# Attention inside a decoder block: where the next head's split, the values and the first output weights stand in the order of work

## The chip, the cores and the metric

The kernel runs on one core of a Trainium2 chip, as one program. The metric is the device time of an execution in microseconds (us); lower is better. The engines are TensorE (PE, matmuls), VectorE (DVE), ScalarE (ACT), GpSimd (POOL) and SyncE (SP), which here only issues DMA transfers. They run side by side and wait for each other through semaphores.

## The reference

One decoder block over 1024 positions with 1024 features, in float32. The mixer has 16 heads of 64 features: 8 choose the 256 best keys of each query by an indexer (DSA), 8 have a forgetting bias (FoX). Cut to what matters:

```python
mod = silu(c) @ ada_w + ada_b                      # 6 vectors of 1024
sh1, sc1, g1, sh2, sc2, g2 = split(mod, 6)
h = rms_norm(x, norm_attn_g) * (1 + sc1) + sh1
q_d, k_d, v_d, iq, ik, iw, q_f, k_f, v_f, f = split(h @ w_in)
o_d = softmax(where(among_best_256, q_d @ k_d.T / 8, -inf)) @ v_d    # per head, rope on q_d, k_d
o_f = softmax(q_f @ k_f.T / 8 + cum_q - cum_k, causal) @ v_f         # per head
y = concat(rms_norm(o_d, dsa_norm_g), rms_norm(o_f, fox_norm_g)) @ w_out
x = x + g1 * y
h = rms_norm(x, norm_ffn_g) * (1 + sc2) + sh2
x = x + g2 * ((silu(h @ w_gate) * (h @ w_up)) @ w_down)
return rms_norm(x, final_norm_g)
```

## The kernel before, in words

Each engine has one program, written out by hand; its order of work is the order of the text, and the only ties between engines are semaphores. The stages are: normalisation, projection and the choice of keys (to 378 us of the span), attention (to 705 us), the output projection and second normalisation, and the feed-forward part with the last normalisation. The change lies in attention.

Attention is a loop over 128 units: 16 heads (numbered 0 to 15; the FoX heads are 0 to 7, the DSA heads 8 to 15) of 8 tiles (0 to 7) of 128 queries each. Tile t has t+1 blocks of keys, so late tiles are larger. For unit s:

- TensorE (`logits`, L1943 to L1945) makes the scores of unit s, turns the exponentials of unit s-2 (`turn`, L1926), and multiplies those of unit s-3 with the values (`values`, L1957). The scores of unit s need VectorE's pass over unit s-2.
- VectorE (`biased`, L1524) adds the bias or the choice and takes the minimum. ScalarE (`expo`, L1015) takes the exponential and copies what TensorE has turned (L1010).
- Queries and keys are split into a high and a low part, for precision. For a head hd, SyncE loads its queries and keys twice over the partitions (`load_qk`, L540, 1 MB into `Qd`, `Kd`). GpSimd's `prepare(hd)` makes two casts (L764, L765) and the low part of the keys (L767, `k_lo`). VectorE's `query_lo(hd)` (L1543, `q_lo`) makes the low part of the queries; it needs both casts, and TensorE needs both low parts for tile 0 of that head. VectorE does `query_lo(hd+1)` at tile 3 of head hd.
- GpSimd does `prepare(0)`, then three memsets (L805, of the sums `g1b`, `g2b`, `mod23`) and two copies that spread the rope angles (L807), then `prepare(hd+1)` in the loop over heads. `prepare(hd)` waits until head hd-2 has made its scores.
- The second part of the modulation vectors is summed along: in heads 4 to 11, at tiles 1, 3, 5 and 7, VectorE adds one block of `ada_w` (`modulation(n)`, L1537). SyncE loads the blocks (`load_mod`, L588, 512 KB into `adar`), two buffers, each as its buffer comes free.
- The values of four heads at a time lie in `Vn` (`load_values(g)`, L531, 1 MB): group 2 (heads 8 to 11) is loaded in SyncE's pass hd = 5, group 3 (heads 12 to 15) in the pass hd = 8, there after a wait for the product of head 7.
- Heads 4 to 6 also turn the DSA rows (`rotate`); the pass hd = 6 of SyncE stores them (L609) and waits for the store before it loads head 8's queries.
- In head 10 VectorE squares the FoX outputs (`square`, L1559), ScalarE takes the root at tile 0 of head 11 (`roots(1)`, L1020, which needs another table of the activation function than the exponential), VectorE inverts it at tile 5 of head 11 (L1591) and scales with it in head 12.
- The output weights are split by GpSimd in heads 12 to 14 (`split_out`, L729, L731). SyncE loads their blocks (L627) after the last queries.

SyncE's passes are one queue: what stands behind a wait waits too. The pass hd is:

```python
load_qk(hd + 2)
if 1 <= hd and hd + 1 < NH:
    load_cum(hd + 1)
if hd == 5:
    load_values(2)
if hd == 8:
    load_values(3)
while n_mod < min(MOD_PER_HEAD * (hd + 1 - MOD_FIRST) + 2, 4 * KT):
    load_mod(n_mod)
    n_mod += 1
```

Of the kernel before, what the change touches and what calls it, by code (L numbers as in the profile page):

```python
# [24 lines left out]
P = 128  # L25
SEQ = 1024
D = 1024
TT = SEQ // P
KT = D // P
DH = 64  # L30
NH = 8
# [157 lines left out]
def build(nc, x, c, positions, ada_w, ada_b, norm_attn_g, w_in, b_forget, dsa_norm_g, fox_norm_g,  # L189
# [14 lines left out]
    with ExitStack() as ctx:  # L204
# [274 lines left out]
        def _(sp):  # L479
# [53 lines left out]
            def load_qk(hd):  # L533
                b, first, row = hd % 2, 0 if hd < NH else 2, hd % NH * DH
                if hd >= 2:
                    sp.wait_ge(k_lo, hd - 1)
                    sp.wait_ge(q_lo, hd - 1)
                for i, dst in enumerate((Qd[b], Kd[b])):
                    for half in range(2):
                        sp.dma_start(dst[half * DH:(half + 1) * DH, :],  # L540
                                     qk_dram[first + i, row:row + DH, :]).then_inc(qk_in[b], 16)
# [56 lines left out]
            for i, dst in enumerate((g1b[0:1, :], mod23[0:1, 0, :], mod23[0:1, 1, :], g2b[0:1, :])):  # L598
                sp.dma_start(dst, ada_b[(2 + i) * D:(3 + i) * D].rearrange("(a n) -> a n", a=1)).then_inc(mod_bias_in, 16)
            n_mod = 0  # L600
            for hd in range(2 * NH - 2):
                if hd == 1:
                    sp.wait_ge(qk_pe, TT)
                    for i in range(2):
                        sp.dma_start(RX[i][:], rope_rows(i)).then_inc(rx_in, 16)
                if hd + 2 == NH:
                    sp.wait_ge(rope_d, 6)
                    for i in range(2):
                        sp.dma_start(rope_rows(i), RX[i][:]).then_inc(rope_out, 16)  # L609
                    sp.wait_ge(rope_out, ROPE_OUT)  # L610
                load_qk(hd + 2)
                if 1 <= hd and hd + 1 < NH:
                    load_cum(hd + 1)
                if hd == 5:
                    load_values(2)
                if hd == 8:
                    load_values(3)
                while n_mod < min(MOD_PER_HEAD * (hd + 1 - MOD_FIRST) + 2, 4 * KT):
                    load_mod(n_mod)
                    n_mod += 1  # L620

            for k in range(KT):
                if k >= 2:
                    sp.wait_ge(w_ready, N_PROJ + k - 1)
                else:
                    sp.wait_ge(md_done, 4 * KT - 1 + k)
                sp.dma_start(adar[:, k % 2, :], w_out[k * P:(k + 1) * P, :]).then_inc(wo_in[k % 2], 16)  # L627


            sp.wait_ge(pv_pe, UNITS)  # L630
# [74 lines left out]
        def _(pool):  # L705
# [95 lines left out]
            pool.wait_ge(cumT_ok, 2)  # L801
            prepare(0)
            pool.wait_ge(pj_pe, NC * TT)
            for dst in (g1b, g2b, mod23):
                pool.memset(dst[:], 0.0).then_inc(md_ms, 1)  # L805
            for i, angle in enumerate((cosT, sinT)):
                pool.tensor_copy(spread[i][:], angle[:].unsqueeze(2).to_broadcast([P, TT, REPS, HALF])).then_inc(spread_ok, 1)  # L807
            for hd in range(2 * NH):
                if hd + 1 < 2 * NH:
                    prepare(hd + 1)  # L810
                    if hd + 1 in ROPE_HEADS:
                        rotate(ROPE_HEADS.index(hd + 1))
                for k in range(KT):
                    if WO_HEAD[k] == hd:
                        split_out(k)
# [49 lines left out]
        def _(act):  # L865
# [157 lines left out]
            for s in range(UNITS + 2):  # L1023
                hd, t = divmod(s, TT)
                if s in ANGLE_UNITS:
                    evac_group(("C", ANGLE_UNITS.index(s)))
                if s in MOD_UNITS:
                    evac_group(("M", MOD_UNITS.index(s)))
                if s == 11 * TT:
                    roots(1)  # L1030
                if s >= 2:
                    for b in range(len(halves(P * ((s - 2) % TT + 1)))):
                        evac_group(("T", s - 2, b))
                if s < UNITS:
                    expo(s)
# [146 lines left out]
        def _(dve):  # L1182
# [383 lines left out]
            def scaled(t, kind):  # L1566

                v = O[:, t, kind * GW:(kind + 1) * GW]
                r = kind * TT + t
                dve.tensor_scalar(v, v, rstd[:, 1, r:r + 1], None, ALU.mult).then_inc(yn_ok, 1)  # L1570
# [3 lines left out]
            dve.wait_ge(pj_pe, NC * TT)  # L1574
            for s in range(UNITS):
                hd, t = divmod(s, TT)
                if t == 3 and hd + 1 < 2 * NH:
                    query_lo(hd + 1)
                biased(s)

                if t == 5 and hd >= 1:
                    normalise(hd - 1)
                if hd == 10:
                    square(t, GW, GW, (2, 1))
                if hd == 12:
                    scaled(t, 1)
                if hd == 15:
                    square(t, 0, GW - LATE, (2, 0))
                if hd == 11 and t == 5:
                    dve.wait_ge(yroot, 1)  # L1590
                    dve.reciprocal(rstd[:, 1, TT:2 * TT], stat[:, 3, TT:2 * TT]).then_inc(yrstd, 1)  # L1591
                    dve.wait_ge(yrstd, 1)
                if MOD_FIRST <= hd < MOD_HEADS and t in MOD_TILES:
                    modulation(len(MOD_TILES) * (hd - MOD_FIRST) + MOD_TILES.index(t))
                advance(CHOICE_LATE.get(s, 0))
# [521 lines left out]
```

## Time and profile before

| | |
|---|---|
| runs shown | 1511.62, 1514.23, 1506.62 us (median 1511.62) |
| profiled execution | 1509.27 us; its span 1507.6 us |
| TensorE busy | 1416.2 us, 94% of the span |
| VectorE, ScalarE, GpSimd busy | 839.3, 666.5, 709.5 us |
| mean granted clock of TensorE | 0.965 of full |
| attention stage | 378 to 705 us |

The profile is one execution, recorded by the hardware. A busy time says how long an engine had an instruction in work; what it waited for stands in the chain, in the groups of waits and in the timelines. In a timeline a row is the start, the duration, the engine, the line, the operation with its output and inputs, and in brackets how long the engine was idle before it and what ended that. Times in the text are microseconds from the start of the span.

### The profile page before, as it was taken

The page shows a single profiled execution, that of the slowest core. Times are in us where ns is not written, and L with a number is a line of the kernel's source. Part 1 is how long each engine was busy: PE and PEld are TensorE (multiplying, and loading weights), DVE is VectorE, ACT ScalarE, POOL GpSimd, SP SyncE. Part 2 cuts the span into 40 slices and gives each one's busy share as a digit, 9 for nine tenths or more (in the row PEclk, how much of TensorE's full clock was granted, in tenths as well). Part 3 has the DMA queues.
Part 4 walks back from the last instruction along what each step waited for, and adds up shares of the span by engine and source line. Part 5 has one row for each costly group of instructions (what it writes and reads, how often), then busy time and mean ns, then how long its engine had stood idle before and what let it go on. Part 6 is the DMA issues. An engine that isn't in the chain of part 4 may idle for free.

```text
span 1507.6 us, 19842 instructions
## 1 busy us (share of the span) xinstructions
PE 1416.2 (94%) x7231; PEld 1205.5 (80%) x7231; DVE 839.3 (56%) x1456; ACT 666.5 (44%) x1274; POOL 709.5 (47%) x455
## 2 busy tenths in 40 slices
PE   1899899999799999998999799999999998999998
PEld 1888678888699988987788688888888886888886
DVE  5634879996567779635455733444433343515414
ACT  4523456541466656656435443333333332423421
POOL 2331312242435322280003998888888873642640
PEclk8899999999899999898899899999999999999999
DMA  9121222241624665520411122222222226643631
GB/s 380 48 74 60 77 78 91 91 150 50 170 63 112 207 201 162 140 78 29 154 43 56 50 90 85 84 84 84 84 85 84 84 71 259 226 150 138 205 126 56
DMA packets 103915, 171.73 MB, mean 114 GB/s; under 512 B 7981, under 2 KB 58341, under 8 KB 102794
## 3 DMA queue, kind: packets, MB, share of 16 engines
q1 hardware_dynamic: 103818, 170.46, 35.2%
q8 instruction: 58, 0.95, 0.3%
q14 instruction: 39, 0.32, 0.1%
HBM read 136.81 MB, written 33.62 MB: 113 GB/s over the span
## 4 chain that ended last, share of the span: by engine, by line
PE 82%; DVE 6%; DMA 4%; issue 2%; ACT 2%; SPq 2%; POOL 1%; DVEq 0%; POOLq 0%; ACTq 0%
PE PS L1783 22%; PE PS L1784 21%; PE PS L1785 21%; PE PS L1957 7%; PE PS L1926 3%; PE PS L1944 2%; PE PS L1945 2%; DMA rawb<-in_w_down_dram 1%; PE PS L1943 1%; DMA adar<-in_ada_w_dram 1%; DVE acc L1228 1%; PE PS L1987 1%; DVE marks_c L1365 1%; DVE XLf L1672 1%; DVE LP L1524 0%
## 5 line engine op out<-in xcount | busy, mean ns | idle before, releaser
L861 POOL TENSOR_TENSOR BS<-rawb,BS 128x1024 fp32r<-128x1024 f32 x44 | 106.9, 2434 | 127.9 <-ACT BS L1144 127.9
L848 POOL TENSOR_TENSOR WS<-WSf,WS 128x512 fp32r<-128x512 f32 x110 | 162.7, 1486 | 0.7 <-ACT WS L1088 0.7
L1088 ACT CAST WS<-WSf 128x512 fp32r<-128x512 f32 x110 | 68.4, 622 | 202.0 <-POOL WSf L838 201.1
L838 POOL TENSOR_TENSOR WSf<-rawg 128x512 f32<-128x512 f32 x55 | 77.3, 1405 | 167.7 <-PE PS L1785 166.5
L1957 PE MATMUL PS<-Vn,PT 128*128 128x64 f32 x1152 | 148.6, 276 | 0.2 <-ACT PT L1010 0.2
L1957 PEld LDWEIGHTS PS<-Vn,PT 128*128 128x128 f32 x1152 | 145.1, 199 | 0.9 <-ACT PT L1010 0.3
L1783 PE MATMUL PS<-BS,AS 128*128 128x512 f32 x352 | 138.0, 392 | 6.5 <-POOL BS L861 6.2
L1783 PE MATMUL PS<-yh,WS 128*128 128x512 f32 x352 | 137.9, 392 | 2.9 <-DVE yl L1644 2.9
L1785 PE MATMUL PS<-yh,WS 128*128 128x512 f32 x352 | 137.7, 391 | 0.0
L1784 PE MATMUL PS<-BS,AS 128*128 128x512 f32 x352 | 137.5, 391 | 0.0
L1784 PE MATMUL PS<-yl,WS 128*128 128x512 f32 x352 | 137.5, 391 | 0.0
L1785 PE MATMUL PS<-BS,AS 128*128 128x512 f32 x352 | 137.4, 390 | 0.0
L1716 DVE TENSOR_TENSOR AS<-rawa,AS 128x512 fp32r<-128x512 f32 x44 | 63.5, 1445 | 127.7 <-ACT AS L1142 127.7
L1015 ACT ACTIVATE LP<-LP,nmin 128x128 f32<-128x128 f32 (+7 forms) x128 | 99.8, 780 | 55.9 <-DVE nmin L1524 53.9
L1010 ACT COPY PT<-PS 128x512 f32<-128x512 f32 (+1 forms) x192 | 85.2, 477 | 63.0 <-PE PS L1926 62.5
L1783 PE MATMUL PS<-XH,WS 128*128 128x512 f32 x264 | 104.6, 396 | 5.6 <-DVE XL L1677 5.6
L1785 PE MATMUL PS<-XH,WS 128*128 128x512 f32 x264 | 104.4, 395 | 0.0
L1784 PE MATMUL PS<-XL,WS 128*128 128x512 f32 x264 | 104.2, 395 | 0.0
L1365 DVE TENSOR_SCALAR_CACHE_REDUCE marks_c<-sel,bis 128x640 f32<-128x640 f32 (+4 forms) x134 | 102.0, 815 | 0.5
L1926 PE MATMUL PS<-ident,LP 128*128 128x128 f32 x576 | 89.2, 283 | 6.2 <-ACT PT L1010 5.2
L764 POOL CAST QT<-Qd 128x1024 fp32r<-128x1024 f32 x16 | 18.1, 1131 | 153.2 <-PE PS L1945 150.8
L949 ACT ACTIVATE PS<-sel,bis 128x896 f32<-128x896 f32 x64 | 67.6, 1056 | 48.6 <-DVE bis L1420 36.9
(306 smaller groups left out, 3516.9 us busy)
## 6 DMA issues: line engine op xcount, KB each, us to landing
rawb<-in_w_down_dram SPq DMA_DIRECT2D x44, 512.0 KB, 3.5
adar<-in_ada_w_dram SPq DMA_DIRECT2D x32, 512.0 KB, 4.4
raw<-in_w_in_dram SPq DMA_DIRECT2D x24, 512.0 KB, 3.9
rawg<-in_w_gate_dram SPq DMA_DIRECT2D x22, 512.0 KB, 4.7
rawu<-in_w_up_dram SPq DMA_DIRECT2D x22, 512.0 KB, 4.3
gu_scratch<-Cu SPq DMA_DIRECT2D x44, 256.0 KB, 2.0
rawa<-gu_scratch SPq DMA_DIRECT2D x44, 256.0 KB, 3.6
ada<-in_ada_w_dram SPq DMA_DIRECT2D x8, 1024.0 KB, 9.4
```

The source lines that it names most:

```text
L838: pool.tensor_tensor(WSf[m % N_SLOT][:], left(i, mat, a), left(i, mat, b), ALU.add if sign > 0 else ALU.subtract).then_inc(ws_sum, 1)
L848: pool.tensor_tensor(lo, WSf[m % N_SLOT][:] if b else left(i, mat, a), hi.bitcast(F32), ALU.subtract).then_inc(ws_ready, 1)
L861: pool.tensor_tensor(b[:, 1, :], rawb[m % 2][:], b[:, 0, :].bitcast(F32), ALU.subtract).then_inc(gb_lo, 1)
L1010: act.copy(PT[:, u % 2, b * BANK:b * BANK + w], src[:, 0:w]).then_inc(tp_ev, 1)
L1015: act.activation(LP[:, u % 3, 0:n], LP[:, u % 3, 0:n], ACT.Exp, bias=nmin[:, u:u + 1], scale=-1.0, accum_out=sums[:, u:u + 1]).then_inc(ex ...
L1088: act.copy(WS[m % N_SLOT][:, 0], src).then_inc(ws_hi, 1)
L1365: did(dve.tensor_scalar(marks[0][:, n_tk % 2, 0:P * (t + 1)], view(t), limit, 0.0, op, ALU.add, accum_out=col(0, t)))
L1783: pe.matmul(dst, left[0], right[0], start=first, stop=False)
L1784: pe.matmul(dst, left[0], right[1], start=False, stop=False)
L1785: return pe.matmul(dst, left[1], right[0], start=False, stop=last)
L1926: last = pe.transpose(dst[:, i * P:(i + 1) * P], src, ident[:])
L1957: last = pe.matmul(PS[:, 6 + hd % 2, t * DH:(t + 1) * DH], PT[:, u % 2, j * P:(j + 1) * P], Vn[(hd // 4) % 2][:, j, cols], start=j == 0, s ...
```

## The change

Five things are moved; no instruction is added or removed.

- GpSimd: `prepare(1)` stands ahead of the memsets and spread copies.
- VectorE: `query_lo(hd+1)` stands at tile 6 of head hd, ahead of `biased`; it was at tile 3.
- ScalarE and VectorE: `roots(1)` at tile 6 of head 11 (was tile 0), its reciprocal at tile 0 of head 12 (was tile 5 of head 11).
- SyncE: values group 2 in the pass hd = 6 (was 5), group 3 in the pass hd = 9 (was 8).
- SyncE: the first two blocks of output weights ahead of head 14's queries (were behind head 15's).

```diff
@@ SyncE
+            def load_out(k):
+                if k >= 2:
+                    sp.wait_ge(w_ready, N_PROJ + k - 1)
+                else:
+                    sp.wait_ge(md_done, 4 * KT - 1 + k)
+                sp.dma_start(adar[:, k % 2, :], w_out[k * P:(k + 1) * P, :]).then_inc(wo_in[k % 2], 16)
...
+                if hd == WO_HEAD[0]:
+                    load_out(0)
+                    load_out(1)
                 load_qk(hd + 2)
                 if 1 <= hd and hd + 1 < NH:
                     load_cum(hd + 1)
-                if hd == 5:
+                if hd == 6:
                     load_values(2)
-                if hd == 8:
+                if hd == 9:
                     load_values(3)
@@ GpSimd
             pool.wait_ge(pj_pe, NC * TT)
+            prepare(1)
             for dst in (g1b, g2b, mod23):
                 pool.memset(dst[:], 0.0).then_inc(md_ms, 1)
...
             for hd in range(2 * NH):
-                if hd + 1 < 2 * NH:
+                if 1 <= hd < 2 * NH - 1:
                     prepare(hd + 1)
@@ ScalarE
-                if s == 11 * TT:
+                if s == 11 * TT + 6:
                     roots(1)
@@ VectorE
-                if t == 3 and hd + 1 < 2 * NH:
+                if t == 6 and hd + 1 < 2 * NH:
                     query_lo(hd + 1)
                 biased(s)
...
                 if hd == 12:
+                    if t == 0:
+                        dve.wait_ge(yroot, 1)
+                        dve.reciprocal(rstd[:, 1, TT:2 * TT], stat[:, 3, TT:2 * TT]).then_inc(yrstd, 1)
+                        dve.wait_ge(yrstd, 1)
                     scaled(t, 1)
...
-                if hd == 11 and t == 5:
-                    dve.wait_ge(yroot, 1)
-                    dve.reciprocal(rstd[:, 1, TT:2 * TT], stat[:, 3, TT:2 * TT]).then_inc(yrstd, 1)
-                    dve.wait_ge(yrstd, 1)
```

How the order of instructions changes at three places. First GpSimd at the start of attention, before (the row with `qk_in1` is the first of `prepare(1)`, the row with `qk_pe` the first of `prepare(2)`):

```order
L805 MEMSET g1b 128x1024 [waits pj_pe]
L805 MEMSET g2b 128x1024
L805 MEMSET mod 128x2048
L807 COPY spread<-cosT 128x1024
L807 COPY spread<-sinT 128x1024
L764 CAST QT<-Qd 128x1024 [waits qk_in1]
L765 CAST KA<-Kd 128x1024
L767 TENSOR_TENSOR KB<-Kd,KA 128x1024 [waits qk_hi]
L764 CAST QT<-Qd 128x1024 [waits qk_pe,qk_in0]
```

and now:

```order
L770 CAST QT<-Qd 128x1024 [waits qk_in1,pj_pe]
L771 CAST KA<-Kd 128x1024
L773 TENSOR_TENSOR KB<-Kd,KA 128x1024 [waits qk_hi]
L812 MEMSET g1b 128x1024
L812 MEMSET g2b 128x1024
L812 MEMSET mod 128x2048
L814 COPY spread<-cosT 128x1024
L814 COPY spread<-sinT 128x1024
L770 CAST QT<-Qd 128x1024 [waits qk_pe,qk_in0]
```

The split of head 1 has gone ahead of five instructions. Second SyncE in the passes hd = 5 and 6, before (`Vn` is the values, `adar` the modulation blocks, `RX` the rotated rows, `bfor_in` the wait for their store):

```order
L531 DMA Vn<-v_scratch 128x8x256 [waits pv_pe]
L588 DMA adar<-in_ada_w_dram 128x1024 [waits md_done] x4
L609 DMA qk_scratch<-RX 16x8x1024 [waits rope_d]
L609 DMA qk_scratch<-RX 16x8x1024
L540 DMA Qd<-qk_scratch 64x1024 [waits q_lo,k_lo,bfor_in]
L540 DMA Qd<-qk_scratch 64x1024
L540 DMA Kd<-qk_scratch 64x1024 x2
L550 DMA CK<-cum_scratch 2x1024 [waits qk_pe]
L551 DMA CQ<-cum_scratch 2x1024
L588 DMA adar<-in_ada_w_dram 128x1024 [waits md_done] x4
```

and now:

```order
L588 DMA adar<-in_ada_w_dram 128x1024 [waits md_done] x4
L616 DMA qk_scratch<-RX 16x8x1024 [waits rope_d]
L616 DMA qk_scratch<-RX 16x8x1024
L540 DMA Qd<-qk_scratch 64x1024 [waits q_lo,k_lo,bfor_in]
L540 DMA Qd<-qk_scratch 64x1024
L540 DMA Kd<-qk_scratch 64x1024 x2
L550 DMA CK<-cum_scratch 2x1024 [waits qk_pe]
L551 DMA CQ<-cum_scratch 2x1024
L531 DMA Vn<-v_scratch 128x8x256 [waits pv_pe]
L588 DMA adar<-in_ada_w_dram 128x1024 [waits md_done] x4
```

The values have moved from ahead of pass 5's modulation blocks to between head 8's queries and pass 6's blocks. Third VectorE in head 6, from tile 5's modulation on, before:

```order
L1537 SCALAR_TENSOR_TENSOR mod<-adar,cact,mod 128x1024 [waits md_done,mod_in0]
L1524 ISA LP,nmin<-PS,strip 128x896 [waits qk_pe,strip_ok,tp_pe]
L1524 ISA nmin 128x1
L1524 ISA LP,nmin<-PS,strip 128x1024 [waits qk_pe,strip_ok,tp_pe]
L1524 ISA nmin 128x1
```

and now:

```order
L1544 SCALAR_TENSOR_TENSOR mod<-adar,cact,mod 128x1024 [waits md_done,mod_in0]
L1550 TENSOR_TENSOR QT<-Qd,QT 64x1024 [waits qk_hi]
L1531 ISA LP,nmin<-PS,strip 128x896 [waits qk_pe,strip_ok,tp_pe]
L1531 ISA nmin 128x1
L1531 ISA LP,nmin<-PS,strip 128x1024 [waits qk_pe,strip_ok,tp_pe]
L1531 ISA nmin 128x1
```

The low query part now stands between tile 5's modulation and tile 6's scores (128x896).

## Rows read from the trace of the kernel before

**Rows 1.** The page, chain of waits, share of the span by engine:

```profile
PE 82%; DVE 6%; DMA 4%; issue 2%; ACT 2%; SPq 2%; POOL 1%; DVEq 0%; POOLq 0%; ACTq 0%
```

**Rows 2.** Waits of TensorE, 378 to 705: total, times, longest:

```profile
PE PS L1943 <- DVE nmin L1524: 7.5, 3, 6.5
PE PS L1926 <- ACT PT L1010: 5.2, 5, 1.7
```

**Rows 3.** Timeline of VectorE in head 0, tile 3:

```profile
388.42 1.22 DVE L1543 TENSOR_TENSOR QT<-Qd,QT 64x1024 fp32r<-64x1024 f32 x1 [6.87 <-POOL KA L765]
```

**Rows 4.** Timeline of TensorE: tile 5 and next tile 0, heads 0 and 6:

```profile
390.43 0.79 PE L1943 MATMUL PS<-CK,CQ 128*128 128x512 f32 x1 [6.47 <-DVE nmin L1524]
...
401.13 0.31 PE L1943 MATMUL PS<-CK,CQ 128*128 128x128 f32 x1
...
510.20 0.47 PE L1943 MATMUL PS<-CK,CQ 128*128 128x512 f32 x1
...
518.96 0.30 PE L1943 MATMUL PS<-CK,CQ 128*128 128x128 f32 x1 [0.59 <-DVE nmin L1524]
```

**Rows 5.** Timeline of GpSimd, 378 to 392:

```profile
378.33 0.95 POOL L805 MEMSET g1b<- 128x1024 f32 x1 [29.46 <-PE PS L1785]
...
386.36 1.04 POOL L764 CAST QT<-Qd 128x1024 fp32r<-128x1024 f32 x1 [2.46 <-DMA Kd<-qk_scratch]
...
388.47 3.41 POOL L767 TENSOR_TENSOR KB<-Kd,KA 128x1024 fp32r<-128x1024 f32 x1
```

**Rows 6.** Timelines of VectorE and TensorE, end of head 11:

```profile
615.75 1.08 DVE L1524 CUSTOM_DVE_ANT_0 LP<-PS,sel 128x896 f32<-128x896 f32 x1
...
618.25 0.31 PE L1944 MATMUL PS<-KA,QT 128*128 128x128 f32 x1
```

**Rows 7.** Timelines of VectorE and TensorE, head 13, tile 3:

```profile
643.99 1.22 DVE L1543 TENSOR_TENSOR QT<-Qd,QT 64x1024 fp32r<-64x1024 f32 x1 [3.01 <-POOL KA L765]
...
646.00 0.50 PE L1944 MATMUL PS<-KA,QT 128*128 128x512 f32 x1 [1.57 <-DVE nmin L1524]
```

**Rows 8.** Timeline of ScalarE at the root, head 11, tile 0:

```profile
597.52 1.28 ACT L1020 ACT_TABLE_LOAD   x1
598.82 0.30 ACT L1020 ACTIVATE stat<-stat,epsc 128x8 f32<-128x8 f32 x1
```

**Rows 9.** Timeline of TensorE at the same place:

```profile
599.64 0.55 PE L1926 MATMUL PS<-ident,LP 128*128 128x128 f32 x3 [1.73 <-ACT PT L1010]
```

**Rows 10.** Windows: busy PE, PEld, DVE, ACT, POOL; PEclk; DMA share; GB/s:

```profile
600.00:612.00 12.00, 12.00 (x59) 11.34 (x58) 5.32 (x9) 6.22 (x15) 0.00 (x0) 0.57 0.70 179
612.00:624.00 12.00, 12.00 (x100) 11.58 (x99) 10.48 (x17) 8.77 (x21) 5.24 (x3) 1.00 0.48 128
560.00:564.00 4.00, 4.00 (x23) 4.00 (x23) 2.05 (x6) 2.17 (x7) 0.00 (x0) 0.57 0.64 182
```

**Rows 11.** SyncE's issues, heads 5 and 7, time to landing; head 5's window:

```profile
483.28 1.09 SPq L540 DMA_DIRECT2D Qd<-qk_scratch  x2
...
L588 SPq DMA_DIRECT2D adar<-in_ada_w_dram x1: 578/578/578, 486.9 to 486.9; - x1
DMA to landing us min/median/max: 8.4/8.4/8.4
...
523.66 1.09 SPq L540 DMA_DIRECT2D Qd<-qk_scratch  x2
...
L588 SPq DMA_DIRECT2D adar<-in_ada_w_dram x1: 583/583/583, 526.1 to 526.1; - x1
DMA to landing us min/median/max: 8.5/8.5/8.5
...
483.00:496.20 13.20, 13.20 (x105) 12.56 (x104) 10.22 (x18) 7.42 (x20) 8.69 (x3) 1.00 0.92 279
```

**Rows 12.** Timeline of VectorE: tile 5's modulation, heads 6 and 8:

```profile
516.52 1.28 DVE L1537 SCALAR_TENSOR_TENSOR mod<-adar,cact,mod 128x1024 f32<-128x1024 f32 x1 [3.06 <-DMA adar<-in_ada_w_dram]
...
553.77 2.00 DVE L1537 SCALAR_TENSOR_TENSOR mod<-adar,cact,mod 128x1024 f32<-128x1024 f32 x1 [2.57 <-DMA adar<-in_ada_w_dram]
```

More of the change, by code:

```diff
@@ L620, in _ @@
                     n_mod += 1
[L622 to L627, printed above, removed]
+            for k in range(2, KT):
+                load_out(k)
             sp.wait_ge(pv_pe, UNITS)
```

## The prediction

> **What bounds the kernel now.** I read the chain of waits on the page first: TensorE holds 82% of it [rows 1]. Only what makes TensorE idle, or run at the lower of its two clock levels (1.2 for 2.4 GHz), can be gained by moving other engines' work. The change touches only the attention stage (378 to 705 us), so I asked next for TensorE's waits there. They are few: 7.5 us in 3 waits for VectorE's score pass, 6.5 us of it one wait, and 5.2 us in 5 waits for ScalarE's copies [rows 2]. Then I followed each wait back in the timelines and read the granted clock around it. "Tile t of head h" names a step; a head takes 15 to 21 us.
>
> **Head 1's split first on GpSimd, and its query part behind tile 6 (removes the 6.5 us wait).** At tile 3 of head 0 VectorE comes to the low query part of head 1. It starts at 388.42 after 6.87 us of idleness, when GpSimd has made both casts [rows 3]. TensorE idles 6.47 us behind it, from 383.96 to 390.43 [rows 4]. GpSimd's casts start at 386.36, and not because of the memsets: it had finished those and idled 2.46 us for the transfer of head 1's keys [rows 5]. So the new place of the split on GpSimd brings nothing by itself; 386.36 stays. What helps is the new place on VectorE. Without the wait, tiles 3, 4 and 5 go through at once. VectorE reaches tile 6 at about 387, waits to 388.4, takes 1.22 us for the part, and has tile 6's scores by 390.7. TensorE needs them for tile 0 of head 1. From tile 5 to the next head's tile 0 it takes 518.96-510.20-0.59 = 8.2 us in head 6; in head 0 it took 401.13-390.43 = 10.7 us, at the low clock at first [rows 4]. So it comes to head 1 at 383.96+8.2 = 392.1. GpSimd's low key part ends at 388.47+3.41 = 391.9 [rows 5], just before. The gain is 6.5+2.5 = 9.0; I take 8.5, since three engines meet within a microsecond there. Bounds: 4 (tile 6 waits instead and the clock falls all the same) and 9.5.
> The memsets and the two spread copies behind them, 5.6 us from 378.33 on (the first stands in [rows 5]), move to 391.9 to 397.5. SyncE waits for the memsets before it loads head 2's queries and keys, so these are issued at about 396.5 and land near 402; GpSimd splits them by 408, and head 2 begins at about 410. Nothing, with 2 us to spare; if that is gone, TensorE idles up to 3 us there (kept for the range).
>
> **The query part behind tile 6 in heads 1 to 14.** The same instruction, 1.22 us, now stands ahead of tile 6's scores and behind what comes at tile 5: a normalisation and, in heads 4 to 11, a modulation that needs a transfer. Where VectorE keeps pace, TensorE has room: in head 11 tile 6's scores begin at 615.75, end 1.08 later, and are first needed at 618.25, with no idle time [rows 6]. I charge 0.5 us for all such heads together, bounds 0 and 3. In head 13 it gains: at tile 3 VectorE waits 3.01 us for GpSimd, which was splitting output weights, and TensorE idles 1.57 us [rows 7]. At tile 6 the casts are done. -1.6.
>
> **First output weights ahead of head 14's queries.** The two transfers wait for modulations 30 and 31 (about 619), and head 14's queries now queue behind them: issued at 620 in place of 611, needed at 635. Nothing. GpSimd splits two output blocks earlier, which helps head 13's wait once more; that is counted already.
>
> **The root at tile 6 of head 11 (was tile 0).** ScalarE loads a table, takes the root and loads the table back. It starts at 597.52 [rows 8], when VectorE is late from head 10's squares, and TensorE idles 1.73 us [rows 9]. The clock then falls: 600 to 612 starts 59 matmuls at 0.57, where 612 to 624 starts 100 [rows 10]. At that rate 59 take 7.1 us, so the stretch costs 4.9. The 1.73 goes. Of the 4.9 I count half, since VectorE's lateness, which stays, may bring the clock down without the root. At the new place the same 2.9 us of ScalarE (two loads of 1.28 and a root of 0.30) delays tile 6's exponential, which is late by the query part anyway: I charge 1.0, bounds 0 and 2. Together -1.7-2.5+1.0 = -3.2.
> In the row the root follows the load at once. The Trainium skill (ScalarE: Activation LUTs, What ACT_TABLE_LOAD costs) adds a drain of 1.38 us to each load of 1.28; by the page the charge at the new place would be up to 2.8 larger, and the gain smaller by that.
>
> **Values one head later.** This is where the change can lose. One 1 MB transfer moves from head 5 to head 6, another from head 8 to head 9. It delays the modulation weight behind it on the same queue, which VectorE wants at tile 5. From the issue of a head's queries to the landing of that weight: head 5, with values, 486.9+8.4-483.28 = 12.0 us; head 7, without, 526.1+8.5-523.66 = 10.9 [rows 11]. So values cost it 1.1 us; against that, 1.05 MB at the 279 GB/s of head 5's whole burst [rows 11] would be 3.8.
> Head 6 is already the worst: its queries wait for the rotated rows to be stored, and VectorE waits 3.06 us for the weight [rows 12]; TensorE idles 1.6. Values now come in front: I take 2.1, between the two. The query part adds 1.2 behind it. TensorE then idles 4.9 us in place of 1.6. In head 8 an idle time of 2.8 was followed by a low clock, 23 matmuls in 560 to 564 for 33 [rows 10], worth 1.2; I add 1.3. +4.6, bounds +1 and +9.
> Head 8: VectorE wants the weight at 551.2 and gets it at 553.77 [rows 12]. Without values it lands 10.9 after its queries' issue at 540.9, at 551.8: a wait of 0.6 for 2.57, but 1.2 of query part: -0.8. Head 9 takes the transfer over: landing 12.0 after the queries, wanted at 10.3 as in head 8, so 1.7, and 1.2 of query part: +2.9. Together +2.1, bounds -3 and +6.
> The Trainium skill (DMA: Bandwidth & Descriptors, Queues, rings and completion order) says that each DMA engine takes descriptors in ring order. By that page the weight would wait for every byte of the values, and the gain would be 4.4 smaller (1.7 in head 6, 2.7 in head 9); head 5's row, only 1.1 above head 7's, speaks for less.
>
> **Sum.** -8.5+0.5-1.6-3.2+4.6+2.1 = -6.1 us on the profiled execution's 1509.27, so 1503.2. The median of the runs shown is 2.35 above that execution; on it the forecast is **1505.5**, 0.4% faster. A measurement of this kernel can tell about 0.5% (7.6 us) from no change.
>
> **Rivals.**
> 1. The moved values are hidden and the full clock stays. For it: head 5 carried the same transfer with no wait of VectorE. Against it: the store in front of head 6's queries, and the short heads from 8 on. -8.5-1.6, the root's 1.7 and 4.9, head 8's 2.8 and 1.2, and +1.0 for the root's new place: -19.7, or 1492.
> 2. Slower: the values in front of head 6's and head 9's weights. The weight waits for all their bytes (3.8 for 2.1 and 1.1, +4.4), each idle time of over 3 us is followed by a low-clock stretch as long as 600 to 612 (4.9 twice for the 1.3, +8.5), and head 10's stretch stays (+2.5): -6.1+15.4 = +9.3, or 1521. It decides once the weight lands over 3 us later than now in both heads. Against it: head 5's row.
> 3. The query part is not hidden at tile 6: 1.22 us in 14 heads, 17.1 for the 4.1 charged so far (0.5, and 1.2 in heads 6, 8 and 9): +6.9, or 1518.5. It needs a VectorE without slack behind tile 5 in all heads; head 11 speaks against it [rows 6].
> 4. The first wait only changes place: VectorE waits at tile 6 for a later transfer and TensorE's clock falls there. The gain of 8.5 shrinks to 4: 1510.
>
> **Numbers.** The forecast, with its own range of 1499 to 1511, has 0.50; rival 1 (with what lies half-way to it) 0.22; rival 2 0.10; rival 3 0.05; rival 4 0.13. The range 1495 to 1515 leaves out the far part of rivals 1, 2 and 3, under 0.2. Faster by over 0.5% (below 1504.1): rival 1 and some third of the forecast, 0.38. Slower by over 0.5% (above 1519.2): half of rivals 2 and 3, 0.07. The rest, 0.55, within 0.5%.
>
> **What the profile after would show.** Right: no idle time of TensorE above 1 us in head 0, and head 1 starting near 392; VectorE waiting 4 us or more for a modulation weight in head 6, 1 to 2 us in head 9, and less than now in head 8; no wait at head 13's tile 3; ScalarE's table loads at tile 6 of head 11. The stage ends 6 us earlier, and everything behind it keeps its length. Wrong: TensorE idle in head 0 in spite of the new place, no longer wait in head 6, or a long low clock where there was none.

## The result and the profile after

The changed kernel takes **1534.3 us** (median of 4 runs, 1525.8 to 1538.8) where the kernel before took 1512.9 beside it: a ratio of 1.0137, 95% interval 1.0074 to 1.0201. It is slower by 21 us. The forecast was 1505.5, and the range ended at 1515. Repeated later it was 1535.2 against 1516.0, a ratio of 1.0121 (1.0067 to 1.0176).

The profiled execution of the changed kernel took 1538.82 us, with a span of 1537.1 and a mean granted clock of 0.957 (before: 1509.27, 1507.6 and 0.965). In its lines the score pass is L1531, the low query part L1550, the modulation L1544, and GpSimd's split L770 to L773.

The chain of waits, by engine, still gives TensorE 82% (before: [rows 1]):

```profile
PE 82%; DVE 7%; DMA 3%; issue 3%; SPq 2%; ACT 2%; POOL 1%; DVEq 0%; POOLq 0%; ACTq 0%
```

So the shares on the page of the profile tell nothing. A window over the attention stage alone does. Its columns are length, TensorE busy time with the number of matmuls, granted clock, DMA share and GB/s. First the kernel before, then the changed one:

```profile
379.00:703.00 324.00, 306.35 (x2266) 0.95 0.47 132
```

```profile
384.00:733.00 349.00, 323.39 (x2270) 0.89 0.44 122
```

The stage is 25 us longer with the same matmuls. TensorE idles 25.6 us in place of 17.7, and is busy 17.0 us longer, because it ran more of them at the lower of its two clock levels (0.50 in the windows is 1.2 GHz, 1.00 is 2.4 GHz). (The stage also begins 5 us later. What stands before it was not touched, and in the repeat it began at 379.9, so that part is variation.)

TensorE's waits in the stage: total, times, longest. They answer to [rows 2].

```profile
PE PS L1950 <- DVE nmin L1531: 8.8, 2, 6.5
PE PS L1951 <- DVE nmin L1531: 7.8, 3, 6.1
PE PS L1933 <- ACT PT L1017: 7.4, 9, 1.1
```

Where there was one wait of 6.5 us for VectorE there are now two, and neither is in head 0. Windows of the changed kernel around its four bad places (head 0 with head 1, then heads 6, 9 and 11) show the clock behind them:

```profile
400.00:404.00 4.00, 1.14 (x5) 0.74 0.05 18
404.00:412.00 8.00, 7.78 (x36) 0.50 1.04 245
412.00:416.00 4.00, 4.00 (x17) 0.55 1.05 229
...
524.00:528.00 4.00, 0.00 (x0) 0.60 0.15 32
528.00:536.00 8.00, 6.15 (x28) 0.50 0.59 174
536.00:540.00 4.00, 4.00 (x26) 0.69 0.97 236
...
588.00:592.00 4.00, 0.00 (x0) 0.71 0.41 131
592.00:600.00 8.00, 6.00 (x27) 0.50 0.45 113
600.00:612.00 12.00, 12.00 (x54) 0.50 0.39 101
612.00:616.00 4.00, 4.00 (x26) 0.81 0.39 131
...
640.00:644.00 4.00, 2.53 (x13) 0.61 0.02 6
644.00:656.00 12.00, 12.00 (x55) 0.50 0.48 131
656.00:660.00 4.00, 4.00 (x25) 0.76 0.00 0
```

A fifth stretch, 702 to 710 at 0.57, is no part of the loss: the kernel before has its like at 671 to 680 (0.62).

**Head 6**, VectorE and the GpSimd row beside it, then the TensorE row that waits. They answer to [rows 12] and to head 6's row in [rows 4]:

```profile
523.61 3.04 DVE L1544 SCALAR_TENSOR_TENSOR mod<-adar,cact,mod 128x1024 f32<-128x1024 f32 x1 [5.80 <-DMA adar<-in_ada_w_dram]
526.68 1.22 DVE L1550 TENSOR_TENSOR QT<-Qd,QT 64x1024 fp32r<-64x1024 f32 x1
527.93 1.09 DVE L1531 CUSTOM_DVE_ANT_0 LP<-PS,strip 128x896 f32<-128x896 f32 x1
...
523.23 2.34 POOL L773 TENSOR_TENSOR KB<-Kd,KA 128x1024 fp32r<-128x1024 f32 x1
...
529.18 0.45 PE L1950 MATMUL PS<-CK,CQ 128*128 128x128 f32 x1 [6.47 <-DVE nmin L1531]
```

Three delays stand in series there. The weight is late by 5.80 us (3.06 before). The modulation behind it takes 3.04 us, where the 32 of them mostly take 1.28; it runs beside GpSimd's subtraction of 523.23 to 525.57 and ends 1.1 us after it. The query part, which stood at tile 3, adds 1.22. **Head 9** shows the same three, with the query part as the most stretched one, again ending 1.1 us after GpSimd's subtraction:

```profile
586.86 1.69 DVE L1544 SCALAR_TENSOR_TENSOR mod<-adar,cact,mod 128x1024 f32<-128x1024 f32 x1 [3.87 <-DMA adar<-in_ada_w_dram]
588.59 3.25 DVE L1550 TENSOR_TENSOR QT<-Qd,QT 64x1024 fp32r<-64x1024 f32 x1
591.87 1.09 DVE L1531 CUSTOM_DVE_ANT_0 LP<-PS,sel 128x896 f32<-128x896 f32 x1
...
587.56 3.19 POOL L773 TENSOR_TENSOR KB<-Kd,KA 128x1024 fp32r<-128x1024 f32 x1
```

This is how lateness feeds on itself. GpSimd starts the split as soon as TensorE has used the old keys (its own idle time ends by TensorE there), so a VectorE that is late meets it. VectorE's instruction then takes longer (1.22 and 3.25 us for the same L1550), and sometimes GpSimd's too (2.34 and 3.19 us for the same L773).

**Head 0.** The wait at tile 3 is gone as forecast. But the memsets and spread copies that GpSimd now runs behind the split (0.96, 0.96, 1.81, 1.43 and 1.04 us) meet a comparison of VectorE (L1464, a step of the choice of keys that is left for the first heads):

```profile
393.81 1.22 DVE L1550 TENSOR_TENSOR QT<-Qd,QT 64x1024 fp32r<-64x1024 f32 x1 [1.19 <-POOL KA L771]
...
396.15 5.14 DVE L1464 TENSOR_SCALAR marks_d<-sel,bis 128x896 f32<-128x896 f32 x1
401.21 1.21 DVE L1531 CUSTOM_DVE_ANT_0 LP<-PS,strip 128x1024 f32<-128x1024 f32 x1
...
397.21 0.96 POOL L812 MEMSET g1b<- 128x1024 f32 x1
398.10 0.96 POOL L812 MEMSET g2b<- 128x1024 f32 x1
399.00 1.81 POOL L812 MEMSET mod<- 128x2048 f32 x1
400.75 1.43 POOL L814 COPY spread<-cosT 128x1024 f32<-128x1024 f32 x1
...
397.33 0.33 PE L1950 MATMUL PS<-CK,CQ 128*128 128x128 f32 x1
...
402.48 0.58 PE L1950 MATMUL PS<-CK,CQ 128*128 128x256 f32 x1 [2.35 <-DVE nmin L1531]
```

Head 1 begins at 397.33, 13.0 us after the stage's start at 384.3 (before: 401.13 in [rows 4], 22.1 after 379.0). Then VectorE's comparison takes 5.14 us, and TensorE waits at head 1's second tile.

### The profile page after: what moved, and what is told of

The parts are those of the page before. It is cut to its first block, busy times and chain, and to the rows that moved or that the text cites. A ratio compares the mean times of both kernels' runs of the same rounds, so it can differ in the third digit from the quotient of the medians.

```text
span 1537.1 us, 19843 instructions
## 1 busy us (share of the span) xinstructions
PE 1435.8 (93%) x7231; PEld 1224.2 (80%) x7231; DVE 843.3 (55%) x1456; ACT 667.4 (43%) x1274; POOL 706.5 (46%) x455
## 4 chain that ended last, share of the span: by engine, by line
PE 82%; DVE 7%; DMA 3%; issue 3%; SPq 2%; ACT 2%; POOL 1%; DVEq 0%; POOLq 0%; ACTq 0%
PE PS L1790 21%; PE PS L1792 21%; PE PS L1791 21%; PE PS L1964 7%; PE PS L1933 4%; PE PS L1951 2%; PE PS L1952 2%; DMA rawb<-in_w_down_dram 1%; DMA adar<-in_ada_w_dram 1%; PE PS L1950 1%; DVE LP L1531 1%; DVE acc L1235 1%; PE PS L1994 1%; DVE marks_c L1372 1%; DVE XLf L1679 1%
## 5 line engine op out<-in xcount | busy, mean ns | idle before, releaser
L1964 PE MATMUL PS<-Vn,PT 128*128 128x64 f32 x1152 | 158.0, 288 | 0.0
L1964 PEld LDWEIGHTS PS<-Vn,PT 128*128 128x128 f32 x1152 | 155.2, 211 | 0.7
L770 POOL CAST QT<-Qd 128x1024 fp32r<-128x1024 f32 x16 | 18.4, 1152 | 214.1 <-PE PS L1952 169.5
L1933 PE MATMUL PS<-ident,LP 128*128 128x128 f32 x576 | 94.5, 295 | 8.5 <-ACT PT L1017 7.4
L1933 PEld LDWEIGHTS PS<-ident,LP 128*128 128x128 f32 x576 | 73.4, 152 | 19.5 <-ACT PT L1017 10.0
```

The costliest lines, as they stand in the source:

```text
L1933: last = pe.transpose(dst[:, i * P:(i + 1) * P], src, ident[:])
L1964: last = pe.matmul(PS[:, 6 + hd % 2, t * DH:(t + 1) * DH], PT[:, u % 2, j * P:(j + 1) * P], Vn[(hd // 4) % 2][:, j, cols], start=j == 0, s ...
```

## The experiments

Theory A: the loss is made of delays in series, a late weight first, with the query part and a stretched instruction behind it. Rivals: the query part at tile 6 alone (B), the root alone (C), the values alone (V), the clash in head 0 (D). All ratios are to the kernel before on the same chip.

### One part undone at a time

Values back at heads 5 and 8:

```
-                if hd == 6:
+                if hd == 5:
                     load_values(2)
-                if hd == 9:
+                if hd == 8:
                     load_values(3)
```

> The changed kernel with the values of groups 2 and 3 loaded at heads 5 and 8 again, as before. Theory A (compounded lateness): the modulation weight that lands late behind the values (waits of 5.80 and 3.87 us in heads 6 and 9) and the query part at tile 6 behind it delay VectorE by more than two tiles, TensorE idles 6 us each time and 14 to 24 us at half clock follow. Without the late weights both stretches go: about 1516 us, with full clock at heads 6 and 9, and the stretch of head 11 still there. Theory B (the query part at tile 6 alone carries the loss): 1530 us or more. Theory C (the root at tile 6 of head 11 carries it): 1530 us or more.

Query part back at tile 3:

```
-                if t == 6 and hd + 1 < 2 * NH:
+                if t == 3 and hd + 1 < 2 * NH:
```

> The changed kernel with the low query part at tile 3 again in every head. Theory A: the late weights stay (waits of 4 to 6 us in heads 6 and 9), but TensorE then waits for the weight alone, without the 1.2 to 3.2 us of the query part behind it: about 1522 us, the low clock behind heads 6 and 9 shorter than 14 and 24 us. Theory B (the query part carries the loss): 1505 to 1510 us, and full clock in heads 6, 9 and 11. Theory C (root): 1530 us or more.

Root back at the start of head 11 (`s == 11 * TT`), its reciprocal back at tile 5:

> The changed kernel with the second roots at the start of head 11 again and their reciprocal at tile 5. Theory A: the root is a third delay in head 11 (2.6 us of table loads beside a weight wait of 1.57 us), worth one stretch of some 18 us at half clock: about 1528 us. Theory C (the root carries the loss): 1512 us. Theory B (query part): 1534 us, unchanged.

Split of head 1 behind the memsets again:

```
-            prepare(1)
             for dst in (g1b, g2b, mod23):
...
-                if 1 <= hd < 2 * NH - 1:
+                if hd + 1 < 2 * NH:
```

> The changed kernel with head 1's split behind the memsets and copies of GpSimd again. Theory A, with the clash in head 0 (GpSimd's memsets beside VectorE's comparison, which took 5.14 us for 0.68, give back what the earlier split gains): the memsets run beside the first tiles, the comparison at tile 6 takes under 1 us, and since the query part stands at tile 6 its split is ready by then anyway: 1526 us, that is 8 us less than the changed kernel. Rival D (the earlier split is a gain and the clash costs nothing that TensorE sees): 1538 us or more.

| changed kernel, but | median us | ratio to before (95%) |
|---|---|---|
| values undone | 1528.1 | 1.0055 (1.0025 to 1.0084) |
| query part undone | 1518.1 | 1.0015 (0.9991 to 1.0038) |
| root undone | 1529.4 | 1.0075 (1.0051 to 1.0099) |
| split undone | 1525.0 | 1.0058 (1.0032 to 1.0085) |

Against the changed kernel's 1.0121 (second table) they give back 0.7, 1.1, 0.5 and 0.6%, 2.8% together, where the whole loss is 1.2%. That points to parts that are not independent, but it is not proof: the 1.0121 is known to 0.55% and counts four times in the sum, and the root's 0.5% can't be told from nothing. The root and the split came as forecast (1528 and 1526 expected), the query part within 4 us (1522). With the values undone theory A, as I had put it, said 1516 and full clock in heads 6 and 9; B and C said 1530 or more, and 1528 came. So taking the moved values away is not enough. In its profiled execution (1533.9, some 6 us above its median, so left out of the table of the account below) two weights are still late, by 3.11 and 1.85 us, as the kernel before had them (3.06 and 2.57), with the query part behind them: in head 6 TensorE waits 2.74 us, and the clock is low from 533 to 551. With the query part undone the weight of head 6 was as late as ever (5.84 us) and the modulation took 3.01, yet the stage was back near its old length:

```profile
380.00:707.00 327.00, 305.27 (x2270) 0.95 0.46 131
```

The split undone cleans head 0. There the comparison takes 1.62 us beside GpSimd's subtraction, and TensorE runs at full clock from 400 to 416, where the changed kernel had 0.74, 0.50 and 0.55:

```profile
394.70 1.62 DVE L1463 TENSOR_SCALAR marks_d<-sel,bis 128x896 f32<-128x896 f32 x1
```

```profile
400.00:416.00 16.00, 15.60 (x114) 1.00 0.50 114
```

### One part alone, on the kernel before

The edits are those of the change, one at a time; the last takes the query part late in head 0 only (`t == (6 if hd == 0 else 3)`).

> The changed kernel once more, beside the partial ones of this call and the kernel before on the same chip. All theories: about 1.4% above the kernel before, some 1535 us.

> The kernel before with the values of groups 2 and 3 moved to heads 6 and 9 and nothing else. Theory A (two delays together make the loss): the weight of head 6 is late by 5.8 us instead of 3.06, TensorE idles some 5 us there and loses some 8 us of clock; head 8's wait goes, head 9 gets one of about 2.5 us: 1518 us, above before by some 5. Theory V (the values alone carry the loss): 1528 us or more.

> The kernel before with the low query part at tile 6 in every head and nothing else. Head 0's wait at tile 3 is gone without a clash (GpSimd's memsets run beside tiles 0 to 3): minus 8 us; in heads 5 to 11 the part of 1.2 us (3.2 beside GpSimd's split) stands behind the weights of tile 5 that are late even before (3.06 and 2.57 us), and the wait reaches TensorE. Theory A: plus 8 to 12 us for these, so 1514 us, the same as before within 0.5%. Theory B (the query part alone carries the loss): 1525 us or more. My forecast's own step (0.5 us): 1505 us.

> The kernel before with the low query part at tile 6 in head 0 alone and at tile 3 in all others. If the only good part of the change is the wait of 6.5 us at head 0's tile 3 with the low clock behind it: 1506 us, 8.5 less than before, and no wait or low clock between 384 and 400 us. If that wait only comes back at a later tile or head: 1513 us.

> The kernel before with the second roots at tile 6 of head 11 and the reciprocal at head 12's first tile, and nothing else. My forecast's step (minus 3.2 us, the idle 2.8 us around 596 and half of the low clock behind it go): 1512 us. Theory C (the root at tile 6 carries part of the loss by itself, since a table load there delays a long tile's exponentials): 1522 us. Theory A (the root costs only where another delay stands beside it, as in the changed kernel's head 11): 1512 to 1516 us.

| kernel | median us | ratio to before (95%) |
|---|---|---|
| the changed kernel again | 1535.2 | 1.0121 (1.0067 to 1.0176) |
| before + values moved | 1517.5 | 1.0013 (0.9990 to 1.0036) |
| before + query part at tile 6, all heads | 1523.6 | 1.0061 (1.0031 to 1.0091) |
| before + query part at tile 6, head 0 only | 1504.5 | 0.9937 (0.9912 to 0.9963) |
| before + root moved | 1512.7 | 0.9972 (0.9944 to 1.0001) |

The values alone cost nothing that can be measured, so V falls. The root alone is a small gain or nothing, so C falls: if it costs at all, it does so only in the changed kernel. The query part is two things. In head 0 it gains 0.6%, and in heads 1 to 14 it loses 1.2%, the difference of two rows, as much as the whole change. My expectation for it (1514) was 10 us too low, nearer B's (1525 or more): by size B is right, and what is left to ask is whether the part costs by itself or only behind a late weight. Its profile at head 8 shows the part in the chain. First VectorE with the part at tile 6 in all heads, and TensorE's window there:

```profile
550.09 1.28 DVE L1537 SCALAR_TENSOR_TENSOR mod<-adar,cact,mod 128x1024 f32<-128x1024 f32 x1 [1.93 <-DMA adar<-in_ada_w_dram]
551.40 1.95 DVE L1543 TENSOR_TENSOR QT<-Qd,QT 64x1024 fp32r<-64x1024 f32 x1
553.38 1.09 DVE L1524 CUSTOM_DVE_ANT_0 LP<-PS,sel 128x896 f32<-128x896 f32 x1
```

```profile
556.00:572.00 16.00, 15.82 (x70) 0.50 0.51 132
```

then the same head with the part late in head 0 only:

```profile
546.25 1.35 DVE L1537 SCALAR_TENSOR_TENSOR mod<-adar,cact,mod 128x1024 f32<-128x1024 f32 x1 [3.22 <-DMA adar<-in_ada_w_dram]
547.52 1.08 DVE L1524 CUSTOM_DVE_ANT_0 LP<-PS,sel 128x896 f32<-128x896 f32 x1
```

```profile
552.00:560.00 8.00, 8.00 (x51) 0.67 0.86 215
```

The weight was later in the second (3.22 for 1.93 us), and still TensorE waited less, 1.69 us against 2.42: the part of 1.95 us is what the edit puts between them. The low clock was shorter too, 8 us at 0.67 against 16 at 0.50, but the edit does not explain that. In the kernel with the root alone, which has nothing changed in head 8, TensorE waited the same 1.69 us there, and the clock stayed low for some 20 us:

```profile
558.25 1.37 DVE L1537 SCALAR_TENSOR_TENSOR mod<-adar,cact,mod 128x1024 f32<-128x1024 f32 x1 [3.21 <-DMA adar<-in_ada_w_dram]
```

```profile
560.00:564.00 4.00, 2.34 (x11) 0.59 0.43 131
564.00:580.00 16.00, 16.00 (x73) 0.50 0.53 133
```

So what the clock adds to one and the same wait varies between executions, here from 1.7 us (the kernel before) to 9.7 us (busy time times one minus the clock), and one profile can't say what an edit is worth. The medians have to.

### The weight ahead of the bulk

If theory A holds, taking away the first delay of the series must disarm the rest. SyncE issues a head's queries and keys, its values where there are any, and only then the weight that VectorE wants at tile 5. This edit issues the weight first, and in head 6 ahead of the wait for the stored rows:

```
                     for i in range(2):
                         sp.dma_start(rope_rows(i), RX[i][:]).then_inc(rope_out, 16)
+                top = min(MOD_PER_HEAD * (hd + 1 - MOD_FIRST) + 2, 4 * KT)
+                if MOD_FIRST < hd and n_mod < top:
+                    load_mod(n_mod)
+                    n_mod += 1
+                if hd + 2 == NH:
                     sp.wait_ge(rope_out, ROPE_OUT)
...
-                while n_mod < min(MOD_PER_HEAD * (hd + 1 - MOD_FIRST) + 2, 4 * KT):
+                while n_mod < top:
                     load_mod(n_mod)
                     n_mod += 1
```

> The kernel before with head 0's query part at tile 6 and, from head 5 on, the weight for tile 5 issued ahead of the next head's queries and keys (and, in head 6, ahead of the wait for the rotated rows). If the weight of tile 5 is late because 1 MB or more of queries, keys and values stands in front of it: no wait of VectorE for a weight over 1 us, full clock around 512 and 552 us, 1498 us (6 less than with the query part alone). If the same bytes only make another weight late (tile 7 or tile 1): 1504 us.

> The changed kernel, all its parts, with the weight for tile 5 issued ahead of the head's queries, keys and values in each head from 5 on. Theory A (the late weight with the query part behind it makes most of the loss): the waits of 5.80 and 3.87 us and the low clock after them go, the clash in head 0 stays: 1518 us. Theory B (the query part beside GpSimd's split delays VectorE by itself): 1530 us.

> The kernel of the second run of this call with the root also at tile 6 of head 11. If the root's move is a gain where nothing else is late there: 2 to 4 us less than that run, 1495 us; if it costs: 2 to 5 us more, 1502 us.

| kernel | median us | ratio to before (95%) |
|---|---|---|
| before + query part late in head 0 + weight ahead | 1495.0 | 0.9848 (0.9825 to 0.9870) |
| the same + root moved | 1494.6 | 0.9845 (0.9823 to 0.9867) |
| the changed kernel + weight ahead | 1505.3 | 0.9916 (0.9890 to 0.9943) |

The changed kernel falls by 2.1% (from 1.0121 to 0.9916), twice what I had expected (the two ratios are from two chips, each against the kernel before on its own), with nothing moved but the order of SyncE's transfers. Its head 6, VectorE, to be read against the rows of head 6 above:

```profile
509.70 1.27 DVE L1549 SCALAR_TENSOR_TENSOR mod<-adar,cact,mod 128x1024 f32<-128x1024 f32 x1
511.00 1.23 DVE L1555 TENSOR_TENSOR QT<-Qd,QT 64x1024 fp32r<-64x1024 f32 x1
512.26 1.09 DVE L1536 CUSTOM_DVE_ANT_0 LP<-PS,strip 128x896 f32<-128x896 f32 x1
```

At tile 5 there is no wait and no stretched modulation, and the query part is harmless. The lateness has not vanished, it has moved to tile 7's modulation:

```profile
515.60 3.05 DVE L1549 SCALAR_TENSOR_TENSOR mod<-adar,cact,mod 128x1024 f32<-128x1024 f32 x1 [1.10 <-DMA adar<-in_ada_w_dram]
```

Behind it stand the short passes of the next head's tiles 0 and 1, and TensorE has no wait for them. In the kernel before with the same cure the weights of tile 7 are late by 1.73 and 2.00 us in two heads, against my expectation of none over 1 us, and behind them TensorE waits at most 0.85 us at a time. (This profiled execution took 1498.3 us, the lowest of its six; that of the repeat below, 1505 us by its span of 1503.6, has 13.0 us idle and 302.0 busy.) TensorE's window over the stage, of this kernel and then of the first row of the table:

```profile
382.00:689.00 307.00, 294.70 (x2263) 0.99 0.50 139
```

```profile
378.00:686.00 308.00, 298.10 (x2268) 0.98 0.50 139
```

### What the rest is

The changed kernel with the weight ahead is still some 10 us above the kernel before with the query part late in head 0 and the same cure (0.7%; without the cure the two are 1.8% apart). Two runs and a repeat, on one chip:

> The changed kernel with the weight ahead (as in the run before) and head 1's split behind the memsets and copies of GpSimd again. If the early split costs by its clash with VectorE's comparison (5.14 us for 0.68, then low clock from 400 to 414) whatever else is late: 1497 us, 8 less than with it early. If the clash costs only in some executions or is taken up: 1503 to 1505 us.

> The changed kernel with the weight ahead and the low query part at tile 3 again in heads 2 to 15 (head 1's stays behind tile 6 of head 0). If the part at tile 6 delays VectorE by itself, with the weights on time (the long tiles 6 and 7, GpSimd's split beside it): 1499 us, 6 less than with it at tile 6. If it costs only behind a late weight: 1505 us, the same.

> The changed kernel with the weight ahead once more, beside the two above on the same chip: 1505 us, 0.8% below the kernel before.

| changed kernel + weight ahead | median us | ratio to before (95%) |
|---|---|---|
| as it is | 1503.7 | 0.9918 (0.9887 to 0.9949) |
| + split behind the memsets | 1500.8 | 0.9908 (0.9879 to 0.9938) |
| + query part at tile 3 from head 1 on | 1501.9 | 0.9906 (0.9881 to 0.9930) |

All three are the same within what was measured. The query part behind tile 6, which cost 1.2% with late weights, now costs some 2 us, which can't be told from nothing; so B holds for the size of the loss and falls as its mechanism: the part costs behind a late weight, and not by itself. The early split's 0.6% shrinks to 3 us, also inside the intervals, and neither run came down as far as its "costs" branch said (1497 and 1499). The clash is not the same in each execution: in the repeat the comparison took 5.13 us, TensorE waited 2.34 and the clock was low from 398 to 416; in the profiled execution before it, of the same kernel, it took 3.36, TensorE waited 0.56 and the clock stayed full. What makes up the rest of the 10 us was not separated. The root adds nothing to the kernel before with the cure (1494.6 for 1495.0); the moved values and the output weights were not tried there.

### The account of the stage

In every profiled execution, idle time is the window's length less TensorE's busy time. The busy time grows with the low clock alone, as the sum below the table shows:

| kernel | idle us | busy us |
|---|---|---|
| before | 17.7 | 306.4 |
| changed | 25.6 | 323.4 |
| changed, query part undone | 21.7 | 305.3 |
| before + values | 22.4 | 311.6 |
| before + query part, all heads | 17.5 | 317.5 |
| before + query part, head 0 | 10.3 | 305.7 |
| before + head 0 + weight ahead | 9.9 | 298.1 |
| the same + root | 6.7 | 297.3 |
| changed + weight ahead | 12.3 | 294.7 |

I took from each busy time the part lost to the clock (busy time times one minus the granted clock, summed over windows of 2 us). In all of the 17 profiled executions 290 to 293 us are left. So the stage's length is 290 to 293 us plus idle time plus clock loss, and nothing else was moved by any of these edits. The +25 us of the change are +8 of idle time and +17 of clock.

## Why the prediction was wrong

The frame was right: only TensorE's idle time and clock count, only the attention stage moves, and everything behind it keeps its length. The sign was wrong. The steps, by the windows (idle time, plus busy time times one minus the clock):

- **Head 0 (forecast -8.5).** The working held up to head 1's first tile: no wait, head 1 at 13.0 us (13.2 forecast), VectorE's part behind 1.2 us of waiting. What failed is the sentence on the memsets and copies, that they cost "Nothing, with 2 us to spare". It asked only whether SyncE's later issue matters, and never what VectorE runs beside them. Idle time and low clock from 400 to 416 are 9 us, where the kernel before lost 11 between 384 and 416. The gain was given back. I also wrote that the new place of the split "brings nothing by itself", and gave it no price; with it undone the changed kernel gains 0.6%. The query part alone in head 0 gains 0.63% (9.6 us), close to the 8.5.
- **Query part at tile 6 (forecast +0.5, bounds 0 and 3).** This step failed worst. Alone on the kernel before, heads 1 to 14 cost 1.2%, some 19 us. I read its price from head 11 [rows 6], a head in which no weight was late, and counted 1.22 us once more where one was. Rival 3 asked for "a VectorE without slack behind tile 5 in all heads". Three heads where TensorE waits behind the part were enough (2.58, 2.42 and 2.01 us with the part alone on the kernel before). Head 13's -1.6 came: the wait is gone.
- **Values, head 6 (forecast +4.6, bounds +1 and +9).** The wait was forecast at 5.2 us and measured 5.80; the idle time of TensorE at 4.9 and measured 6.47. Missing is the stretch of the modulation by 1.76 us. The clock was charged 1.3 us, from head 8's stretch of 4 us in [rows 10]; here it stayed low from 524 to 540. Together some +10.
- **Values, heads 8 and 9 (forecast +2.1, bounds -3 and +6).** Head 8's wait went, as forecast. In head 9 the weight was late by 3.87 for the forecast 1.7, the query part took 3.25 for 1.22, and the clock was low until 616. From 584 to 616 that is 7.0 us idle and 9.8 of clock, where I had +2.9 in all. The values alone on the kernel before cost 0.13%, less than my terms for them. They are dear only with the query part behind them.
- **Ring order.** The Trainium skill's rule (DMA: Bandwidth & Descriptors, Queues, rings and completion order) would have made the waits 6.9 in head 6 and 4.4 in head 9; the row of head 5 made them 5.2 and 1.7. Measured are 5.80 and 3.87. Head 9 speaks for the Trainium skill's rule, head 6 lies between.
- **Root (forecast -3.2).** Alone it gave -0.3% (-4 us, with an interval that just takes in no change): that agrees with the forecast. In the changed kernel it is a fourth delay in head 11, whose weight is 1.57 us late: idle time and low clock from 636 to 660 are 11 us, where the kernel before lost 8 between 592 and 616. Undoing it gains 0.5%, which is within the noise, but its profile has no low clock in head 11. The root starts as its table load ends here too (a load of 1.28 us at 634.85, the root at 636.14), so the rows show nothing of the larger charge that the prediction mentions.
- **Output weights (0).** They were not tried alone.
- **Rival 2**, at 0.10, was the mechanism: the weight late in heads 6 and 9, idle time, then low clock. Its price, +9.3, was under half of what came, because it took the query part as one more 1.22 us and each low stretch as 12 us long. Its condition was too strict as well: in head 6 the weight came 2.7 us later than before, not over 3. It lacked what carries most of the loss, the query part and the stretched instructions behind a late weight, and the memsets in head 0.

The error beneath all of these is one: the costs were summed as if independent, each read in a place where nothing else was late. The clock was priced from one stretch of one execution each time, and the same wait can cost several times that.

## What to carry to other kernels

Before moving an instruction, list what it will stand behind: an instruction put behind a wait that already reaches the bounding engine costs its full time in each such place, plus what the lateness makes the engines beside it collide with, plus the clock. Here 1.2 us in each head was worth 1.2% with late weights in three of them, and nothing measurable with the weights on time. When a small transfer with a due time queues behind bulk transfers that are due a head later, reorder the queue first. That alone gave 2.1% to the changed kernel and about 0.9% to the kernel before with the query part late in head 0, which itself gave 0.6%; the best version was 1494.6 us, 1.55% below before.

## What the runs showed of the hardware

- **GpSimd's memsets hold up a comparison of VectorE through several instructions.** The 128x896 TENSOR_SCALAR takes 0.68 us with GpSimd idle, 1.62 beside one subtraction of 3.42, and 5.14 beside a subtraction and three memsets back to back; it ended 0.5 us after the last memset. The Trainium skill (SBUF — State Buffer, Who interferes with whom) says that a TENSOR_SCALAR in a mode that uses both of VectorE's ports and a GpSimd instruction exclude each other by a lock that is held for a whole instruction, so that the later one waits until the first has finished. The trace agrees on the exclusion, and shows more than one instruction's wait: three memsets passed ahead of the waiting comparison. Of the eight profiled executions with the early split, six show this (4.84 to 5.14 us); in the other two the comparison took 3.36 us, ended 0.5 us after the second memset, and the third took 2.28 us for 1.81.
- **Modulations and query parts stretch beside GpSimd's split:** 3.04 for 1.28 us and 3.25 for 1.22. In both, and in the 1.95 us of the kernel with the query part alone, VectorE's instruction ends 1.1 us after GpSimd's, about the time that it takes alone: it too waits for a whole instruction. The prediction used the unstretched rows.
- **The clock's price is not in proportion to the idle time.** Counted from the wait on and in windows of 2 us, in the changed kernel 6.5 us of waiting in head 6 go with 16 us below full clock, 6.1 us in head 9 with 26 us, although TensorE was busy throughout 600 to 616, and 3.0 us of idle time in head 11 with 18 us. One wait of 1.69 us in head 8 goes with 4 us (before), 8 us (part late in head 0) and 22 us (root alone). The clock also fell where TensorE had been busy without a gap for 10 us: from 702 in the changed kernel, 8 us at 0.57. What decides the length was not settled by these runs.
